# The attention stage of a decoder step: the order in which SyncE begins page loads, where the last eight value pages lie, and the place of the last gate half on TensorE

## The chip, the cores and the metric

The kernel runs as one program on one core of a Trainium2 chip. The metric is the device time of one execution in microseconds (us). The engines are named PE (TensorE), DVE (VectorE), ACT (ScalarE), POOL (GpSimd) and SP (SyncE, which here only begins transfers). PEld is the weight load of TensorE.

## The reference, cut to what matters

One step of a two-layer decoder trunk for a prompt of 512 tokens and 8 sample sequences of 4 tokens. In layer 0 a projection makes q, k, v, forget values and the inputs of a gated convolution. The prompt attends to itself; each sample sequence attends to its 16 cached pages (128 tokens each) and its own 4 tokens:

```
k_all = concat([k_pool[page_table].reshape(bsz, p_len, h, d), k_new], axis=1)
v_all = concat([v_pool[page_table].reshape(bsz, p_len, h, d), v_new], axis=1)
...
s = einsum('bqhd,bkhd->bhqk', q, k) * (HEAD_DIM ** -0.5) + (cq - ck)
p = softmax(s, axis=-1)
return einsum('bhqk,bkhd->bqhd', p, v)
```

An output projection, a ConvFFN, a Conformer convolution module and a second ConvFFN follow; the change does not touch them. Everything is float32; a product with a weight is made as three passes over high and low parts.

## The kernel before, in words

After the q, k, v projection comes a stage of NROUND = 20 rounds, written out in full for each engine. 8 sequences x 16 pages are 128 key pages and 128 value pages of 256 KB. Keys come in groups of GRP = 8 pages, in two buffers (k_grp, slots 0 and 1). Values come page by page, in eight buffers (v_pg). In round n the engines do this:

- PE scores key group n (score_group, L1898, for n < 16), counts it in s_sp, multiplies four value pages (value_page, L1952; the eight pages of a round are 8(n-4) to 8(n-4)+7) right behind it, turns the scores back (keys_back, L1906), scores the prompt's block 2n (block_score, L1969, counted in s_s), computes one or two gate halves (gate_half, L2019, 24 products each: half the columns of one slab of the convolution's projection), multiplies the other four value pages, and sums exponentials (exp_sums, L1937) and picks heads (own_heads, L1959). Each value page used is counted in s_pvp. Before a sequence's first value page PE waits until DVE has read the result of the sequence before (s_oev, counted by values, L1395), and multiplies its new values (L1948).
- DVE transposes key group n+1 in two halves (key_turned, L1262), reads scores and gate halves (L1414), makes sums.
- SP begins the transfers, in program order, each behind its own wait. In round n these are: the row cb of sums for a prompt head (L518, even rounds; it waits for DVE's L1324), the eight pages of key group n+2 (L457, waits s_sp >= n+1), in rounds 0 and 1 the outputs of turned rows, four value pages for PE's round n+1 (L467, each waits until its buffer's last page is counted in s_pvp), a gate weight in some rounds (L473), and the other four value pages.

Page ids are read from a table in SBUF into registers of SP, eight at a time, by page_id (L444), ahead of a group's first key page:

```
if n // GRP not in ids:
    ...
    ids[n // GRP] = nc.values_load_multi_w_load_instructions(
        page_row[0:1, at:at + GRP], engines=(mybir.EngineType.SP,), min_val=0, max_val=NPOOL - 1)[1]
```

Rounds 16 to 19 have no key groups. Round 17 computes the gate halves q = 21 and 22, round 18 the last one, 23. In round 18 PE uses value pages 112 to 119 and in round 19 pages 120 to 127; SP begins the latter behind s_pvp >= 113 to 120. Then the output projection starts (L1768 in `gemm(ph["out"], ...)`, behind L2091, which turns a small tail that DVE copies at L1508). POOL subtracts for the low part of its weights (L664), one slab after gate half 22, one after 23, one after s_pvp reaches 128.

Of the kernel before, what the change touches and what calls it, by code (L numbers as in the profile page):

```python
# [11 lines left out]
ds = bass.ds  # L12

P = 128
# [8 lines left out]
PG = 16  # L23
NPOOL = 160
# [9 lines left out]
KS, VS = 2, 8  # L34
# [6 lines left out]
NPAGE = NB * PG  # L41
GRP = 8
NGRP = NPAGE // GRP
LAG = 4
# [110 lines left out]
def build(nc, a, o):  # L155
# [6 lines left out]
    with ExitStack() as ctx:  # L162
# [58 lines left out]
        w_top = lambda at: at + 2 * DC * P * 4  # L221
        k_grp = [place(f"k_grp{n}", [P, GRP, 4 * P], F32, at)[0] for n, at in enumerate((R0, w_top(raw_at)))]
        own, _ = place("own", [P, P], F32, R0 + 16384)
        v_at = [w_top(wl_at) + n * 2048 for n in range(4)] + [R1, R1 + 2048, qkv_at + 11 * CH, ss_at + 6144]
# [98 lines left out]
        s_k = [[sem(f"k{n}_{half}") for half in range(2)] for n in range(KS)]  # L323
        s_v = [sem(f"v{n}") for n in range(VS)]
        s_ow, s_owr = sem("picked"), sem("picked_read")
        s_stc, s_clr, s_sel = sem("four_copied"), sem("banks_cleared"), sem("selectors")
# [79 lines left out]
        def _(sp):  # L406
# [31 lines left out]
            def page_id(n):  # L438

                if n // GRP not in ids:  # L440
                    if not ids:
                        sp.wait_ge(s_pg, 16)
                    at = n - n % GRP
                    ids[n // GRP] = nc.values_load_multi_w_load_instructions(  # L444
                        page_row[0:1, at:at + GRP], engines=(mybir.EngineType.SP,), min_val=0, max_val=NPOOL - 1)[1]
                return ids[n // GRP][n % GRP]
# [13 lines left out]
            def value_page(n):  # L460

                at = page_id(n)
                if n >= VS:
                    sp.wait_ge(s_pvp, n - VS + 1)
                elif n in (4, 5, 6, 7):
                    sp.wait_ge(s_kd[n - 4], 16)
# [57 lines left out]
            for n in range(NROUND):  # L524
                if n % 2 == 0 and n // 2 < NH:
                    head_cum(n // 2)
                if n + 2 < NGRP:
                    for j in range(GRP):
                        key_page(GRP * (n + 2) + j)
                for r in sum(ROWS_IN.get(n, ()), ()):  # L530
                    rows_written(r)
                values_at = GRP * (n - LAG + 1)
                if 0 <= values_at < NPAGE:
                    for j in range(4):
                        value_page(values_at + j)
                for q in halves_in(n):
                    if q % 2 == 0 and q // 2 + 2 < 12:
                        gate_load(q // 2 + 2)
                if 0 <= values_at < NPAGE:
                    for j in range(4, GRP):  # L540
                        value_page(values_at + j)
                if n == 15:
                    out_load(0)
# [1203 lines left out]
        def _(pe):  # L1747
# [192 lines left out]
            def value_page(n):  # L1940

                b, p = n // PG, n % PG
                if p == 0:
# [3 lines left out]
                    for c in range(4):  # L1947
                        mm(bank[0][32 * c:32 * c + 8, 0:P], pr[0:TS, b % 2, PG, c * 8:c * 8 + 8],  # L1948
                           s_row[:, 1, c * P:(c + 1) * P], start=True, stop=False)
                pe.wait_ge(s_v[n % VS], 16 * (n // VS + 1))  # L1950
                for c in range(4):
                    ins = mm(bank[0][32 * c:32 * c + 8, 0:P], pr[:, b % 2, p, c * 8:c * 8 + 8],  # L1952
                             v_pg[n % VS][:, c * P:(c + 1) * P], start=False, stop=p == PG - 1)
                ins.then_inc(s_pvp, 1)
# [74 lines left out]
            for n in range(NROUND):  # L2029
# [15 lines left out]
                for r in early:  # L2045
                    rows_turned(r)
                if values_at >= 0:
                    for j in range(4):
                        value_page(values_at + j)
# [13 lines left out]
                for r in late:  # L2063
                    rows_turned(r)
                for q in first:
                    gate_half(q, n)
# [185 lines left out]
```

## Time and profile before

| what | value |
| --- | --- |
| median of 3 runs | 1518.27 us (1516.08 to 1519.36) |
| profiled execution | 1527.78 us, its span 1525.9 us |
| PE busy | 1440.1 us (94%) |
| DVE, ACT, POOL busy | 744.6, 473.0, 587.1 us |
| mean granted clock of TensorE | 0.971 of full speed |
| DMA | 192.56 MB, mean 126 GB/s |

The profiled execution is 9.51 us above the median of the three runs. All positions in time below are microseconds from the start of its span. Busy time is the time in which an engine executes something; "idle before" is the gap ahead of an instruction, with what released it, and "issue" there means that the profile shows nothing the engine waited for.

### The profile page before, as it was taken

To read this page: it belongs to the slowest core of one execution; us is meant where nothing else is said; L and a number is where in the kernel's file an instruction comes from. 1 tells how busy PE (TensorE), PEld (TensorE's weight loads), DVE (VectorE), ACT (ScalarE), POOL (GpSimd) and SP (SyncE) were. 2 spreads that over 40 slices of the span, in tenths; PEclk is the share of its full clock that TensorE was granted. 3 is DMA by queue.
4 is the path that set the end of the run, shared out by engine and by line. 5 is a ranking of instruction groups with operands and counts; after the bars stand their busy time and mean duration, and the time that the engine had idled before them with its cause. 6 is when DMAs were issued, how large, how long until landed. Compare 5 with 4: busy or idle time off the path is not lost. (4 is left out here: it accounts for less than half of the span.)

```text
span 1525.9 us, 34946 instructions
## 1 busy us (share of the span) xinstructions
PE 1440.1 (94%) x13997; PEld 1326.6 (87%) x13997; DVE 744.6 (49%) x1258; ACT 473.0 (31%) x678; POOL 587.1 (38%) x321
## 2 busy tenths in 40 slices
PE   6998898899799999999999999986999999999998
PEld 5896666666689999999999987864999999999998
DVE  5654766677443544203443369988345441044411
ACT  5374222222134222312223331116443322222221
POOL 3312222222232645445444344430435444445441
PEclk9999988999989999999999999997999999999999
DMA  5416777987732332233322446560313323323222
GB/s 177 125 52 217 244 250 256 316 281 232 237 100 69 100 93 69 84 97 96 89 70 61 131 124 158 145 159 15 109 56 92 93 70 94 107 79 91 62 78 73
DMA packets 246375, 192.56 MB, mean 126 GB/s; under 512 B 12129, under 2 KB 205106, under 8 KB 246186
## 3 DMA queue, kind: packets, MB, share of 16 engines
q1 hardware_dynamic: 244753, 188.71, 40.6%
q10 hardware_dynamic: 1373, 1.84, 0.5%
q8 instruction: 77, 1.26, 0.3%
q0 software_dynamic: 144, 0.52, 0.1%
q14 instruction: 28, 0.23, 0.0%
HBM read 173.03 MB, written 6.04 MB: 117 GB/s over the span
## 5 line engine op out<-in xcount | busy, mean ns | idle before, releaser
L664 POOL TENSOR_TENSOR w_l<-w_raw,w_h 128x1024 fp32r<-128x1024 f32 (+2 forms) x195 | 432.9, 2222 | 447.6 <-ACT w_h L791 418.8
L1768 PE MATMUL banks<-xa_h,w_h 128*128 128x272 f32 x1856 | 388.2, 290 | 4.5 <-DVE tmp L1590 3.3
L1768 PE MATMUL banks<-xa_h,w_l 128*128 128x272 f32 x1856 | 384.9, 289 | 0.0
L1768 PE MATMUL banks<-xa_l,w_h 128*128 128x272 f32 x1856 | 383.6, 288 | 0.0
L1768 PEld LDWEIGHTS banks<-xa_h,w_h 128*128 128x128 f32 x1856 | 293.3, 189 | 6.8 <-issue 5.5
L1768 PEld LDWEIGHTS banks<-xa_l,w_h 128*128 128x128 f32 x1856 | 292.6, 189 | 0.0
L1768 PEld LDWEIGHTS banks<-xa_h,w_l 128*128 128x128 f32 x1856 | 290.5, 189 | 0.0
L791 ACT ACTIVATE w_h<-w_raw 128x1024 fp32r<-128x1024 f32 (+2 forms) x193 | 185.1, 961 | 182.5 <-PE banks L1768 182.2
L1768 PE MATMUL banks<-h_h,w_h 128*128 128x272 f32 x960 | 202.4, 292 | 8.1 <-DVE h_l L1737 8.0
L1768 PE MATMUL banks<-h_h,w_l 128*128 128x272 f32 x960 | 200.7, 291 | 0.0
L1768 PE MATMUL banks<-h_l,w_h 128*128 128x272 f32 x960 | 200.2, 290 | 0.0
L1529 DVE TENSOR_TENSOR x<-banks,x 128x544 f32 (+1 forms) x48 | 34.8, 725 | 271.5 <-PE banks L1768 271.5
L1768 PEld LDWEIGHTS banks<-h_h,w_h 128*128 128x128 f32 x960 | 153.2, 191 | 10.0 <-issue 7.5
L1768 PEld LDWEIGHTS banks<-h_l,w_h 128*128 128x128 f32 x960 | 153.2, 191 | 0.0
L1768 PEld LDWEIGHTS banks<-h_h,w_l 128*128 128x128 f32 x960 | 152.0, 191 | 0.0
L738 POOL TENSOR_TENSOR sr<-sl,r_all 128x544 f32<-128x544 f32 x44 | 59.8, 1360 | 232.8 <-ACT sl L1022 232.8
L1022 ACT ACTIVATE sl<-cv 128x544 f32<-128x544 f32 x44 | 29.0, 659 | 276.8 <-DVE cv L1585 276.7
L685 POOL TENSOR_SCALAR sb<-sb,small 128x128 f32<-128x128 f32 (+3 forms) x32 | 34.7, 1083 | 180.0 <-DVE small L1336 180.0
L1152 DVE TENSOR_TENSOR gate<-banks,r_all 128x544 f32<-128x544 f32 x44 | 31.8, 724 | 110.5 <-PE banks L1768 104.7
L1590 DVE TENSOR_TENSOR tmp<-banks,sr 128x544 f32<-128x544 f32 x44 | 31.9, 725 | 107.5 <-POOL sr L738 107.5
L1262 DVE STREAM_TRANSPOSE k_grp<-k_grp 128x2048 f32<-128x2048 f32 x32 | 73.5, 2298 | 0.4 <-DMA k_grp<-in_cache_k 0.4
L1576 DVE SCALAR_TENSOR_TENSOR cv<-gate,params,cv 128x511 f32<-128x511 f32 x88 | 66.1, 751 | 12.7
(286 smaller groups left out, 1698.4 us busy)
## 6 DMA issues: line engine op xcount, KB each, us to landing
w_raw<-in_w_up SPq DMA_DIRECT2D x88, 512.0 KB, 3.6
k_grp<-in_cache_k SPq DMA_DIRECT2D x128, 256.0 KB, 4.1
v_pg<-in_cache_v SPq DMA_DIRECT2D x128, 256.0 KB, 5.2
w_raw<-in_w_in SPq DMA_DIRECT2D x24, 512.0 KB, 6.5
w_raw<-in_w_down SPq DMA_DIRECT2D x32, 384.0 KB, 3.1
w_raw<-in_w_pw SPq DMA_DIRECT2D x24, 512.0 KB, 4.1
w_raw<-in_w_down SPq DMA_DIRECT2D x32, 320.0 KB, 3.1
w_raw<-in_w_out SPq DMA_DIRECT2D x8, 512.0 KB, 6.3
```

What stands on the lines that cost most here:

```text
L664: g.tensor_tensor(w_l[:, slot, 0:n], w_raw[:, slot, 0:n], w_h[:, slot, 0:n].bitcast(F32), ALU.subtract).then_inc(s_lo, 1)
L685: g.tensor_scalar(sb[:, k % 2, 0:n], sb[:, k % 2, 0:n], rinv[:, w:w + 1], None, ALU.mult).then_inc(s_pn, 1)
L738: g.tensor_tensor(sr[:, j // 2, :], sl[:, j // 2, :], r_all[:, :], ALU.mult)\
L791: A(w_h[:, slot, 0:n], w_raw[:, slot, 0:n], ACT.Copy).then_inc(s_hi, 1)
L1022: A(sl[:, b, :], cv[:, b, :], ACT.Silu).then_inc(s_sl, 1)
L1152: V.tensor_tensor(halves(dst), gview(b), halves(r_all[:, :]), ALU.mult).then_inc(s_free, 1)
L1262: V.transpose(k_grp[slot][:, at, :].rearrange("p g x -> p (g x)"), k_grp[slot][:, at, :].rearrange("p g x -> p (g x)")).then_inc(s_tk, 1)
L1529: V.tensor_tensor(halves(flat(x[:, ds(m, 1), :])), gview(q % 2), halves(flat(x[:, ds(m, 1), :])), ALU.add).then_inc(s_xnew, 1)
L1576: V.scalar_tensor_tensor(yp, gate[:, b, 0:TP - n], w, yp, ALU.mult, ALU.add)\
L1590: V.tensor_tensor(halves(tmp[:, b, :]), gview(1), halves(sr[:, b, :]), ALU.mult).then_inc(s_free, 1)
L1768: ins = mm(out[:, half, 0:HT], w, v[:, half * HT:(half + 1) * HT], start=first and t == 0 and n == 0, stop=last and t == phase.tiles - 1 a ...
```

## The change

It has four parts.

1. page_id reads the same ids, and leaves out the check of each against 0 and 159.
2. In each round SP's order becomes: four key pages, the turned rows (rounds 0 and 1), four value pages, then a wait for s_s >= 2n+1 (the prompt's block 2n is scored), the other four key pages, the gate weight, the other four value pages.
3. Value pages 120 to 127 go to v_last, which is key buffer 0, free once group 14 is scored (s_sp >= 15). SP begins them in round 15. PE waits for them in two lots of four.
4. Gate half 23 stands ahead of the first value page of round 18 on PE.

```diff
+        v_last = k_grp[(NGRP - 2) % KS]
...
+        s_vl = [sem(f"v_last{n}") for n in range(2)]
...
                     ids[n // GRP] = nc.values_load_multi_w_load_instructions(
-                        page_row[0:1, at:at + GRP], engines=(mybir.EngineType.SP,), min_val=0, max_val=NPOOL - 1)[1]
+                        page_row[0:1, at:at + GRP], engines=(mybir.EngineType.SP,), min_val=0, max_val=NPOOL - 1,
+                        skip_runtime_bounds_check_because=...)[1]
...
                 at = page_id(n)
+                if n >= NPAGE - GRP:
+                    sp.wait_ge(s_sp, NGRP - 1)
+                    sp.dma_start(v_last[:, n % GRP, :], a["cache_v"][0, ds(at, 1)].rearrange("a k h d -> (a k) (h d)"))\
+                      .then_inc(s_vl[n % GRP // 4], 16)
+                    return
...
-                if n + 2 < NGRP:
-                    for j in range(GRP):
-                        key_page(GRP * (n + 2) + j)
-                for r in sum(ROWS_IN.get(n, ()), ()):
-                    rows_written(r)
-                values_at = GRP * (n - LAG + 1)
-                if 0 <= values_at < NPAGE:
-                    for j in range(4):
-                        value_page(values_at + j)
-                for q in halves_in(n):
-                    if q % 2 == 0 and q // 2 + 2 < 12:
-                        gate_load(q // 2 + 2)
-                if 0 <= values_at < NPAGE:
-                    for j in range(4, GRP):
-                        value_page(values_at + j)
+                values_at = GRP * (n - LAG + 1)
+                for half in range(2):
+                    if half and n + 2 < NGRP:
+                        sp.wait_ge(s_s, 2 * n + 1)
+                    if n + 2 < NGRP:
+                        for j in range(4 * half, 4 * half + 4):
+                            key_page(GRP * (n + 2) + j)
+                    if not half:
+                        for r in sum(ROWS_IN.get(n, ()), ()):
+                            rows_written(r)
+                    else:
+                        for q in halves_in(n):
+                            if q % 2 == 0 and q // 2 + 2 < 12:
+                                gate_load(q // 2 + 2)
+                    if 0 <= values_at < NPAGE - GRP:
+                        for j in range(4 * half, 4 * half + 4):
+                            value_page(values_at + j)
                 if n == 15:
+                    for j in range(GRP):
+                        value_page(NPAGE - GRP + j)
                     out_load(0)
...
-                pe.wait_ge(s_v[n % VS], 16 * (n // VS + 1))
+                if n < NPAGE - GRP:
+                    pe.wait_ge(s_v[n % VS], 16 * (n // VS + 1))
+                else:
+                    pe.wait_ge(s_vl[n % GRP // 4], 64)
+                page = v_pg[n % VS] if n < NPAGE - GRP else v_last[:, n % GRP, :]
...
+                if n == NROUND - 2:
+                    half_read(last_half(n, 1))
+                    for q in first:
+                        gate_half(q, n)
                 if values_at >= 0:
                     for j in range(4):
                         value_page(values_at + j)
...
-                for q in first:
+                for q in first if n < NROUND - 2 else ():
                     gate_half(q, n)
```

The order of SP's instructions at the start of round 4 before the change; cb is the row of sums, k_grp a key page, "ISA x16" the sixteen instructions of the check, "ISA" ahead of a key page its address:

```order
L518 DMA cb<-cum_rows 128x512 [waits p_read]
L444 TENSOR_LOAD page_row
L444 ISA x16
L457 ISA [waits page_scored]
L457 DMA k_grp_86<-in_cache_k 128x512
```

The same engine from there on with the change, up to the fifth key page (the row with "p_scored" is the new wait):

```order
L527 DMA cb<-cum_rows 128x512 [waits p_read]
L446 TENSOR_LOAD page_row
L461 ISA [waits page_scored]
L461 DMA k_grp_86<-in_cache_k 128x512
...
L476 DMA v_pg_89<-in_cache_v 128x512 [waits page_valued]
L476 DMA v_pg_90<-in_cache_v 128x512 [waits page_valued]
L476 DMA v_pg_91<-in_cache_v 128x512 [waits page_valued]
L476 DMA v_pg_92<-in_cache_v 128x512 [waits page_valued]
L461 ISA [waits p_scored]
L461 DMA k_grp_86<-in_cache_k 128x512
```

The check's sixteen instructions are gone and the first four value pages stand between the two halves of the key group.

PE in rounds 18 and 19 before the change, with buffer names (v_pg0 to v_pg7 the value pages, s_row the new values; the rows of L2019 are products of gate half 23, of which 24 stand there):

```order
L1948 MATMUL banks<-s_row_84,pr_72 8x128 x4
L1952 MATMUL banks<-v_pg0_89,pr_72 8x128 x4
L1952 MATMUL banks<-v_pg1_90,pr_72 8x128 x4
L1952 MATMUL banks<-v_pg2_91,pr_72 8x128 x4
L1952 MATMUL banks<-v_pg3_92,pr_72 8x128 x4
L2019 MATMUL banks<-xa_h_50,w_h_55 128x288
...
L1952 MATMUL banks<-v_pg4_93,pr_72 8x128 x4
```

And with the change, from the same place to the end of the stage:

```order
L2036 MATMUL banks<-xa_h_50,w_l_56 128x288
L1961 MATMUL banks<-s_row_84,pr_72 8x128 x4
L1969 MATMUL banks<-v_pg0_89,pr_72 8x128 x4
...
L1969 MATMUL banks<-v_pg7_96,pr_72 8x128 x4
L1950 MATMUL banks<-ones_58,small_77 8x1 x4
L1976 MATMUL banks<-small_77,own_88 128x16
L1969 MATMUL banks<-k_grp0_86,pr_72 8x128 x32
```

The gate half stands ahead of the new values' products, and the last eight pages are read from the key buffer in one piece of 32 products.

## Rows read from the trace of the kernel before

**Rows 1.** The page: busy us by engine; one group: busy, mean ns | idle before.
```profile
PE 1440.1 (94%) x13997; PEld 1326.6 (87%) x13997; DVE 744.6 (49%) x1258; ACT 473.0 (31%) x678; POOL 587.1 (38%) x321
...
L664 POOL TENSOR_TENSOR w_l<-w_raw,w_h 128x1024 fp32r<-128x1024 f32 (+2 forms) x195 | 432.9, 2222 | 447.6 <-ACT w_h L791 418.8
```

**Rows 2.** Stretches: us, busy PE, PEld, DVE, ACT, POOL, PEclk, DMA share, GB/s.
```profile
203.90:223.60 19.70, 17.13 (x240) 11.79 (x239) 9.97 (x20) 3.43 (x8) 3.27 (x3) 0.74 0.84 291
223.60:238.50 14.90, 14.31 (x277) 10.91 (x276) 11.46 (x22) 4.25 (x8) 3.70 (x3) 1.00 0.73 239
238.50:258.40 19.90, 16.71 (x240) 11.42 (x239) 11.68 (x24) 3.54 (x8) 4.07 (x4) 0.74 0.85 287
...
287.10:306.70 19.60, 16.58 (x281) 12.70 (x283) 11.75 (x22) 4.31 (x8) 4.50 (x3) 0.83 0.87 300
306.70:319.90 13.20, 12.87 (x243) 8.68 (x244) 9.31 (x19) 3.32 (x8) 3.27 (x3) 1.00 0.68 222
319.90:337.30 17.40, 15.69 (x277) 12.30 (x276) 11.62 (x22) 4.85 (x9) 3.72 (x3) 0.90 1.03 352
...
350.20:368.20 18.00, 16.02 (x277) 12.28 (x276) 12.53 (x23) 4.25 (x8) 3.98 (x3) 0.91 0.63 217
424.90:430.00 5.10, 5.10 (x30) 5.10 (x29) 3.73 (x6) 2.67 (x5) 2.35 (x1) 0.66 0.35 106
```

**Rows 3.** PE's timeline, rounds 5 and 14: start, duration, row, [idle before].
```profile
210.17 0.61 PE L1952 MATMUL banks<-v_pg,pr 128*8 128x128 f32 x6 [2.57 <-issue]
...
350.17 2.62 PE L1898 MATMUL banks<-k_grp,q_blk 32*8 32x256 f32 x122
354.51 0.61 PE L1898 MATMUL banks<-k_grp,q_blk 32*8 32x256 f32 x6 [1.72 <-issue]
```

**Rows 4.** DMA queues between 350.0 and 352.5: packets, MB, share of 16 engines.
```profile
q1 hardware_dynamic: 1068, 0.92, 107.2%
q8 instruction: 1, 0.02, 2.2%
```

**Rows 5.** SP's timeline in round 4, then the instructions of L444.
```profile
191.12 0.33 SPq L518 DMA_DIRECT2D cb<-cum_rows  x1
194.27 5.24 SPq L457 DMA_DIRECT2D k_grp<-in_cache_k  x8
199.61 4.26 SPq L467 DMA_DIRECT2D v_pg<-in_cache_v  x8
...
L444 SPq FUSED_REGOPS  x128: 147/147/188, 43.0 to 338.7; - x128
```

**Rows 6.** PE's timeline, rounds 17 to 19 and the first product of the output projection.
```profile
396.29 0.37 PE L2019 MATMUL banks<-xa_h,w_h 128*128 128x288 f32 x1 [0.91 <-DVE sc_b L1372]
...
399.55 0.28 PE L2019 MATMUL banks<-xa_h,w_h 128*128 128x256 f32 x1
...
407.36 0.40 PE L1948 MATMUL banks<-s_row,pr 32*8 32x128 f32 x8 [3.83 <-DVE own L1395]
...
414.50 0.21 PE L1937 MATMUL banks<-ones,small 128*8 128x1 f32 x8
...
414.97 1.06 PE L1952 MATMUL banks<-v_pg,pr 128*8 128x128 f32 x32
417.51 0.41 PE L1952 MATMUL banks<-v_pg,pr 128*8 128x128 f32 x8 [1.49 <-DMA v_pg<-in_cache_v]
...
421.05 0.61 PE L1952 MATMUL banks<-v_pg,pr 128*8 128x128 f32 x8 [1.60 <-DMA v_pg<-in_cache_v]
...
424.89 0.80 PE L1768 MATMUL banks<-h_h,w_h 128*128 128x272 f32 x2
```

**Rows 7.** DVE's timeline in round 17.
```profile
406.75 0.47 DVE L1395 TENSOR_SCALAR own<-banks,small 128x64 f32<-128x64 f32 x2
```

**Rows 8.** Value pages begun by SP between 403.4 and 404.7.
```profile
L467 SPq DMA_DIRECT2D v_pg<-in_cache_v x3: 379/379/380, 403.4 to 404.3; - x3
...
DMA to landing us min/median/max: 4.3/4.5/4.7
```

More of the change, by code:

```diff
@@ L444, in page_id @@
                     ids[n // GRP] = nc.values_load_multi_w_load_instructions(
-                        page_row[0:1, at:at + GRP], engines=(mybir.EngineType.SP,), min_val=0, max_val=NPOOL - 1)[1]
+                        page_row[0:1, at:at + GRP], engines=(mybir.EngineType.SP,), min_val=0, max_val=NPOOL - 1,
+                        skip_runtime_bounds_check_because="a page table holds ids of the pool's pages, and each page's "
+                                                          "DMA checks its address by itself")[1]
                 return ids[n // GRP][n % GRP]
@@ L526, in _ @@
                     head_cum(n // 2)
-                if n + 2 < NGRP:
-                    for j in range(GRP):
-                        key_page(GRP * (n + 2) + j)
-                for r in sum(ROWS_IN.get(n, ()), ()):
-                    rows_written(r)
-                values_at = GRP * (n - LAG + 1)
-                if 0 <= values_at < NPAGE:
-                    for j in range(4):
-                        value_page(values_at + j)
-                for q in halves_in(n):
-                    if q % 2 == 0 and q // 2 + 2 < 12:
-                        gate_load(q // 2 + 2)
-                if 0 <= values_at < NPAGE:
-                    for j in range(4, GRP):
-                        value_page(values_at + j)
-                if n == 15:
+                values_at = GRP * (n - LAG + 1)
[15 more added lines that the diff above has]
+                            value_page(values_at + j)
+                if n == 15:
+                    for j in range(GRP):
+                        value_page(NPAGE - GRP + j)
                     out_load(0)
@@ L1949, in value_page @@
                            s_row[:, 1, c * P:(c + 1) * P], start=True, stop=False)
-                pe.wait_ge(s_v[n % VS], 16 * (n // VS + 1))
+                if n < NPAGE - GRP:
[3 more added lines that the diff above has]
+                page = v_pg[n % VS] if n < NPAGE - GRP else v_last[:, n % GRP, :]
                 for c in range(4):
                     ins = mm(bank[0][32 * c:32 * c + 8, 0:P], pr[:, b % 2, p, c * 8:c * 8 + 8],
-                             v_pg[n % VS][:, c * P:(c + 1) * P], start=False, stop=p == PG - 1)
+                             page[:, c * P:(c + 1) * P], start=False, stop=p == PG - 1)
                 ins.then_inc(s_pvp, 1)
```

## The prediction

> **What bounds the kernel now.** First the page: PE is busy 94% of the span, so it is the bound nearly everywhere [rows 1]. What a change to SP's queue can bring are PE's remaining gaps and what they cost behind them. Next the stretches by round: PE's work repeats every two rounds, and rounds of one kind should last alike. They don't. Odd round 11 takes 13.20 us, odd rounds 5 and 7 take 19.70 and 19.90; even round 6 takes 14.90, rounds 10, 12 and 14 take 19.60, 17.40 and 18.00 [rows 2]. Over the undisturbed round of their kind that is 6.5, 6.7, 4.7, 2.5 and 3.1, together 23.5 us. In the long rounds the granted clock averages 0.74 to 0.91, in rounds 6 and 11 it is 1.00: a gap is followed by a stretch at the lower of the two levels.
>
> Then PE's timeline at such a gap: in round 5 it stands 2.57 us before the last products of a value quartet, "issue"; in round 14 it stands 1.72 us after 122 of the 128 equal products of one score group, where no semaphore is waited for at all [rows 3]. So something other than data is late. The DMA queues just before show the ordinary queue at 107% of 16 engines, and beside it one packet of the instruction queue; its 2.2% of 16 engines over 2.5 us are 0.9 us [rows 4]. I read it as PE's instructions arriving late through engines that are full of pages. The score group, with a weight load for each of its 128 products in 2.6 us, is where PE uses up instructions fastest, and the gap falls in or just behind it.
>
> Last the end of the stage: PE stands 3.83 us for DVE's `own` before round 18, 1.49 and 1.60 us for the last value pages, and starts the output projection at 424.89 [rows 6].
>
> **The end of the stage (parts 3 and 4).** Before, PE is through with round 17 at 407.36 - 3.83 = 403.53 and starts the projection at 424.89, 21.36 us later [rows 6]. After, step by step: at 403.53 gate half 23 follows; its twin, half 21, took 399.55 - 396.29 = 3.26 [rows 6], so 406.79. Its bank was freed in round 17 before `own`, in DVE's order. `own` is written at 406.75 to 407.22 [rows 7] and PE went on at 407.36 then, and will again: 0.57 of the 3.83 us stay. New values 0.40 and two quartets of 1.06 (the row at 414.97) give 409.88 at full clock; the small products 414.97 - 414.50 = 0.47 give 410.35 [rows 6]; eight pages in one piece, 2 x 1.06, give 412.47. From there to the projection, own_heads, DVE's tail and L2091 stay as they were: before, 424.89 - (421.05 + 0.61) = 3.23. Sum 415.70, against 424.89: **9.2 us** gained.
>
> What hides what: pages 120 to 127 are begun in round 15, some 20 us ahead of use, so their landing is covered. Pages 116 to 119 are not moved, and are now wanted at 408.8: they were begun by 404.3 and landed in 4.3 to 4.7, so at 409.0 for the last [rows 8]; PE uses it as the fourth, at 409.6, with 0.6 to spare. POOL's subtraction behind half 23 starts beside DVE's `own` now. Should they hinder each other, the loss is one POOL operation, 2.2 us on the mean [rows 1]. Eight more page loads stand ahead of SP's first output weight and of pages 104 to 107: 8 x 0.38 = 3.0 us by the issue time of a page [rows 8]. Those four pages were begun about a round ahead of use (13.2 us or more [rows 2]), and the output weights are split only in rounds 17 and 18, so I price both at nothing. Bounds of the end: 9.2 - 2.2 - 0.6 = 6.4 below; above, the projection's first 5.10 us ran at 0.66 [rows 2], and would at full clock be 1.7 shorter: 10.9.
>
> **The ids (part 1).** The check goes: 16 of the instructions of each group, 8 of which take 0.147 us, so at least 1.2 us a group [rows 5]. The gap between cb's end at 191.45 and the first key page at 194.27 is 2.8 us, and holds the load of ids too [rows 5]; I take 2.0 off it. SP is on no path by itself. What moves is when the DMA engines get their work: in even rounds 2 us sooner. In odd rounds the ids are read ahead of the wait for the scores, and little moves.
>
> **The bursts (part 2).** Before, the value pages of round 4 were begun in one run from 199.61 to 203.87 [rows 5], 2 MB in front of round 5's score group and its gap at 207.6 (210.17 - 2.57). With the change four of them are begun in front of the second half of the keys, at about 194.27 - 2.0 + 5.24/2 = 194.9, and only the four that wait for PE's second quartet remain. So about 1 MB less, and everything 2 us sooner, is in the engines when PE's instructions run short. The bytes are the same, and the rate stays near what the engines give: 287 to 352 GB/s in long rounds [rows 2]. That is why I don't expect every gap to go; in rounds as close as 10 and 12 the pages of one round meet those of the next however they are ordered. The new wait, s_s >= 2n+1, holds up behind it four key pages, the gate weight and the last value quartet. The quartet waits for PE anyway, and later; the keys' second half is turned by DVE in the middle of the next round; half a round (6.6 us or more) stands between, and 4 pages need 2.6 of it on SP (half of 5.24 [rows 5]) and 4.7 to land [rows 8], begun in the first third of the round before. Nobody waits.
>
> Its worth outside the profile: the three runs have a median 9.51 below the profiled one, so of the 23.5 us perhaps 14.0 are there at all. Rounds 5 and 7, where the runs of pages shrink, hold 13.2/23.5 = 56%, 7.9 us. Between nothing and 7.9 I take half, **4.0 us**.
>
> The Trainium skill speaks against this term: Runtime: NRT & Kernel Launch, section Instruction fetch mechanics, says that the sequencer streams 16 KiB blocks by its own DMA queue and that this is mostly hidden. The size agrees with the 0.02 MB packet [rows 4]; by its rule the gaps of rows 3 are no fetches, and SP's order would bring nothing.
>
> Sum: 1518.27 - 9.2 - 4.0 = 1505.1 us. In the profiled execution it would be 1527.78 - 13.2 = 1514.6, or less if rounds 5 and 7 lose all 13.2.
>
> **Rivals.**
> - *All gaps of the rounds go.* 14.0 instead of 4.0: 1495.1; from 7.9, 1501.2. For it: the gaps are tied to a full queue. Against: rounds 10, 12, 14 keep as many bytes per us.
> - *Only the end gains.* PE's gaps have another cause, or shift with the pages: 1509.1. For it: no row shows the packet's own wait, and whether a round is hit looks like chance (11 is not). The rule above gives this case.
> - *The end gains little.* Another wait takes the place of the 3.83 us, such as pages 116 to 119 or `own` behind POOL; only the 3.1 us for the last pages are won, and nothing in the rounds: 1515.2. For it: the margin of 0.6 us. Against: it would have to eat the whole gate half.
> - *Slower: the spread pages meet PE's instructions in every round.* Now pages are begun in four places, and one lot follows PE's first quartet directly. A hit costs 6.5 us (round 5). The end's 9.2 are used up from the second additional hit on; four more would be 26 - 9 = 17 slower, 1535; two more, 1522. For it: rounds 6 and 11 run at full clock now and have something to lose. Against: fewer pages in a lot, and those begun earlier.
>
> **How the numbers follow.** Likeliest, 0.44: end and half of the two rounds, 1505.1, its own range 1501.2 to 1509. All or most gaps go: 0.22 (1495 to 1501). Only the end: 0.22 (1509 to 1512 with its lower bound, 1518.3 - 6.4 = 1511.9). End gains little: 0.07 (1512 to 1517). Slower: 0.05. The range 1496 to 1512 leaves out a small part of the second case and the last two, under 0.2. Within 0.2% (about 3 us, what a measurement of this kernel can tell) means 1515.2 to 1521.3: 0.04, from the fourth case and the mildest hits. Faster: 0.92. Slower: 0.04.
>
> **What the profile after would show.** PE goes from half 23's last product to the new values with under 1 us idle; pages 120 to 127 as one run of about 2.1 us with no idle for DMA; the projection starts some 9 us nearer to the end of round 17. In the rounds, the first key page of even rounds is begun within 1 us of cb's end, and rounds 5 and 7 last nearer to 13.2 than to 19.7 with the clock at 1.00. I am wrong if PE shows new idle before the quartets of rounds 16 to 18, if DVE's transpositions wait for keys, or if the "issue" gaps keep their number and only stand elsewhere.

## The result, and the profile after

| | before | with the change |
| --- | --- | --- |
| median, timed side by side (6 runs each) | 1517.17 us | 1502.2 us |
| profiled execution, its span | 1527.78, 1525.9 us | 1501.65, 1499.7 us |
| mean granted clock | 0.971 | 0.982 |
| start of round 4's score group | 189.51 | 188.16 |
| PE through with round 17 | 403.53 | 393.99 |
| start of the output projection | 424.89 | 405.36 |
| from there to the end of the span | 1101.0 | 1094.3 |

The ratio of the two kernels' times is 0.9913, its 95% interval [0.9885, 0.9941]: faster by 13.2 us (9.0 to 17.4). The medians in the table lie 15.0 apart; gains below are by the ratio unless medians are named. The two profiled executions lie 26.2 us apart in their spans. The table splits this: 1.35 ahead of round 4, 8.2 in rounds 4 to 17 (214.0 to 205.8), 10.0 from there to the projection (21.36 to 11.37), 6.7 behind it. The last is in code that the change doesn't touch. In the profiled executions of the experiments below it is 1092 to 1095, and 1100.9 in one: I count it as scatter between executions and no part of the gain.

First the page, against [rows 1]. PE does the same 13997 products in 12.8 us less, at a mean clock that is a little higher:

```profile
PE 1427.3 (95%) x13997; PEld 1317.4 (88%) x13997; DVE 712.8 (48%) x1258; ACT 473.0 (32%) x678; POOL 590.7 (39%) x321
```

PE's timeline from round 17 to the projection, against [rows 6] (start, duration, row, idle before). The first row is the last value quartet of round 17; 24 products of the gate half follow it, of which the first and the last stand here.

```profile
392.93 1.06 PE L1969 MATMUL banks<-v_pg,pr 128*8 128x128 f32 x32
393.92 0.40 PE L2036 MATMUL banks<-xa_h,w_h 128*128 128x288 f32 x1
...
397.09 0.29 PE L2036 MATMUL banks<-xa_h,w_l 128*128 128x288 f32 x1
397.88 0.40 PE L1961 MATMUL banks<-s_row,pr 32*8 32x128 f32 x8 [0.50 <-DVE own L1408]
398.21 2.01 PE L1969 MATMUL banks<-v_pg,pr 128*8 128x128 f32 x64
400.04 0.21 PE L1950 MATMUL banks<-ones,small 128*8 128x1 f32 x8
...
400.50 1.93 PE L1969 MATMUL banks<-k_grp,pr 128*8 128x128 f32 x64
403.04 0.40 PE L1976 MATMUL banks<-small,own 128*128 128x16 f32 x2 [0.60 <-DVE own L1408]
404.99 0.61 PE L2112 MATMUL banks<-ident,tail_a 128*18 128x128 f32 x4 [1.56 <-DVE tail_a L1521]
405.36 0.50 PE L1781 MATMUL banks<-h_h,w_h 128*128 128x272 f32 x2
```

The gate half stands where PE stood 3.83 us; 0.50 us of that wait is left. The four pages 116 to 119 follow without a gap, and so do pages 120 to 127: the three waits for DMA of [rows 6], 1.49 and 1.60 among them, are gone.

SP's timeline in round 4, against [rows 5]: a burst of eight key pages and one of eight value pages have become four of four, and the first key page is begun 0.90 us behind cb's end (191.00 - 190.10), where it was 2.82. It can't be begun sooner now, because it waits for round 4's scores, which end at 188.16 + 2.67 = 190.83.

```profile
189.77 0.33 SPq L527 DMA_DIRECT2D cb<-cum_rows  x1
191.00 1.88 SPq L461 DMA_DIRECT2D k_grp<-in_cache_k  x4
192.98 1.80 SPq L476 DMA_DIRECT2D v_pg<-in_cache_v  x4
195.59 2.12 SPq L461 DMA_DIRECT2D k_grp<-in_cache_k  x4
199.65 1.76 SPq L476 DMA_DIRECT2D v_pg<-in_cache_v  x4
```

Rounds 5, 6, 7, 10, 12 and 14, against [rows 2] (us, busy PE, PEld, DVE, ACT, POOL, granted clock, DMA share, GB/s), and behind them the first 5.1 us of the projection:

```profile
202.50:215.80 13.30, 12.71 (x241) 8.71 (x240) 10.01 (x20) 3.43 (x8) 3.27 (x3) 1.00 0.83 291
215.80:233.90 18.10, 15.71 (x284) 11.98 (x290) 11.67 (x22) 4.25 (x8) 3.78 (x3) 0.91 0.93 310
233.90:247.40 13.50, 12.53 (x240) 8.58 (x239) 11.45 (x24) 3.54 (x8) 3.95 (x4) 1.00 0.82 283
277.90:297.50 19.60, 16.77 (x282) 12.73 (x285) 11.74 (x22) 4.31 (x8) 4.50 (x3) 0.83 0.83 277
310.70:326.50 15.80, 14.09 (x277) 10.93 (x276) 11.67 (x22) 4.85 (x9) 3.70 (x3) 1.00 1.06 394
339.40:357.20 17.80, 16.08 (x283) 11.73 (x287) 12.61 (x23) 4.25 (x8) 4.04 (x3) 0.90 0.63 216
405.40:410.50 5.10, 5.10 (x31) 5.10 (x30) 3.73 (x6) 2.95 (x5) 2.08 (x1) 0.67 0.36 106
```

Rounds 5 and 7 are down from 19.70 and 19.90 to 13.30 and 13.50. But round 6 is up from 14.90 to 18.10 and round 8 from 15.1 to 16.7. Of the 12.8 us that two rounds gave, 4.8 went back in the rounds behind them. Whether the change did this is asked below, under "The same code, other rounds".

PE's gaps in rounds 5, 6 and 14, against [rows 3]. Each gap stands before the last products of a group of equal ones, and waits for no semaphore:

```profile
205.12 1.04 PE L1969 MATMUL banks<-v_pg,pr 128*8 128x128 f32 x26
206.75 0.40 PE L1969 MATMUL banks<-v_pg,pr 128*8 128x128 f32 x6 [0.59 <-issue]
...
219.08 0.84 PE L1969 MATMUL banks<-v_pg,pr 128*8 128x128 f32 x22
222.04 1.01 PE L1969 MATMUL banks<-v_pg,pr 128*8 128x128 f32 x10 [2.13 <-issue]
...
339.63 2.37 PE L1911 MATMUL banks<-k_grp,q_blk 32*8 32x256 f32 x102
343.47 0.61 PE L1911 MATMUL banks<-k_grp,q_blk 32*8 32x256 f32 x6 [1.46 <-issue]
```

An fp32 product leaves two such rows of products, so a quartet of pages has 32 and a score group 128. Count rows from the start of a round's score group (even rounds have 16 more rows between scores and pages, odd rounds none). In rounds 6, 8, 10, 12 and 14 the gap stands after 166, 155, 144, 133 and 122 rows; in rounds 5, 7 and 9 after 154, 143 and 132. Every two rounds it comes 11 rows earlier, in the kernel before too, and no data is due at such places. Rounds 4 and 11 have small ones of the same kind (0.3 to 0.4 us after 176 and 120 rows). Only the lengths differ: 0.59, 2.13, 0.97, 2.08, 1.07, 2.57, 1.44 and 1.46 us for rounds 5 to 10, 12 and 14, where before it was 2.57, 0.33, 3.19, 0.48, 0.74, 2.75, 1.44 and 1.72.

What PE waits for can be read from the DMA view. In rounds 5 to 14 of the kernel before (203.88 to 368.23) the instruction queue moved 21 packets of 16 KB, while PE left 2576 records of products and as many of weight loads (first the queue's line, then that of the window):

```profile
q8 instruction: 21, 0.34, 0.8%
203.88:368.23 164.35, 148.98 (x2576) 108.32 (x2576) 112.35 (x208) 40.19 (x83) 38.32 (x30) 0.90 0.81 276
```

That is one packet for 5152 / 21 = 245 PE instructions, two packets a round. Narrow windows of the same view give the moment at which a packet begins. The last one ahead of each gap's end:

| round | before: packet begins, PE goes on | with the change |
| --- | --- | --- |
| 5 | 207.75, 210.17 | 204.26, 206.75 |
| 6 | 225.64, 228.05 | 219.58, 222.04 |
| 7 | 242.57, 244.94 | 235.80, 238.03 |
| 14 | 352.06, 354.51 | 341.21, 343.47 |

Every time PE goes on 2.2 to 2.5 us after the packet began. The same holds for 85 of the 87 gaps of this kind of 0.2 us and more between 200 and 360 us in the traces of all kernels of this document (the other two: 2.85 and 3.11, behind packets that took 1.4 and 1.6 us; the median packet of the kernel before takes 0.95). So the gaps are PE waiting for its own instructions, and a gap is longer the later its packet begins.

### The profile page after: what moved, and what is told of

The parts are those of the page before. It is cut to its first block, busy times and chain, and to the rows that moved or that the text cites. A ratio compares the mean times of both kernels' runs of the same rounds, so it can differ in the third digit from the quotient of the medians.

```text
span 1499.7 us, 34690 instructions
## 1 busy us (share of the span) xinstructions
PE 1427.3 (95%) x13997; PEld 1317.4 (88%) x13997; DVE 712.8 (48%) x1258; ACT 473.0 (32%) x678; POOL 590.7 (39%) x321
## 4 chain that ended last, share of the span: by engine, by line
PE 84%; DVE 7%; issue 3%; ACT 3%; DMA 1%; POOL 1%; SPq 0%; ACTq 0%; DVEq 0%; POOLq 0%
PE banks L1781 65%; PE banks L2036 5%; PE banks L2203 2%; PE banks L1911 2%; PE banks L1969 2%; PE banks L2009 1%; PE banks L1986 1%; PE banks L1919 1%; DVE k_grp L1275 1%; DVE suf L1217 1%; PE banks L1813 1%; DVE ssum L1183 1%; PE banks L1996 1%; PE banks L2155 0%; DMA x_rows<-in_x_sample 0%
## 5 line engine op out<-in xcount | busy, mean ns | idle before, releaser
L677 POOL TENSOR_TENSOR w_l<-w_raw,w_h 128x1024 fp32r<-128x1024 f32 (+2 forms) x195 | 439.1, 2253 | 429.5 <-ACT w_h L804 408.8
L1589 DVE SCALAR_TENSOR_TENSOR cv<-gate,params,cv 128x511 f32<-128x511 f32 x88 | 66.1, 751 | 12.8
```

What stands on the lines that cost most here:

```text
L677: g.tensor_tensor(w_l[:, slot, 0:n], w_raw[:, slot, 0:n], w_h[:, slot, 0:n].bitcast(F32), ALU.subtract).then_inc(s_lo, 1)
L1589: V.scalar_tensor_tensor(yp, gate[:, b, 0:TP - n], w, yp, ALU.mult, ALU.add)\
```

## The experiments

Each kernel was timed against the kernel before on the same chip, and the ratios have 95% intervals. Three groups were each timed together: end_only, rounds_only, after_shift128 and before_shift128 (before: 1515.14 us); ids_only, bursts_only, after_light_pages and after_shift64 (1515.96); the last four (1515.33). Parts are numbered as in the section on the change.

**The end alone and the rounds alone.** end_only has parts 3 and 4 (pages 120 to 127 into v_last, gate half 23 first), rounds_only has parts 1 and 2.

```diff
 end_only: before, with
+                    sp.dma_start(v_last[:, n % GRP, :], ...).then_inc(s_vl[n % GRP // 4], 16)
+                if n == NROUND - 2:
+                    half_read(last_half(n, 1))
+                    for q in first:
+                        gate_half(q, n)
 rounds_only: before, with
+                        skip_runtime_bounds_check_because=...
+                    if half and n + 2 < NGRP:
+                        sp.wait_ge(s_s, 2 * n + 1)
```

> Parts 3 and 4 alone: pages 120 to 127 in the key buffer, gate half 23 ahead of round 18's values; the ids are checked and SP keeps the order of before. My theory (the end is worth about 9.2 us by itself, measured 10.0 between the two profiled executions, the rest of the gain comes from the rounds): 8 to 11 us faster than before, and in the profile the same 11.4 us from the end of round 17 to the first product of the output projection as in the changed kernel; rounds 5 and 7 as long as before (19 to 20 us) if the profile catches them so. Rival (the whole gain is the end, the rounds only scatter): 12 to 14 us faster.

> Parts 1 and 2 alone: unchecked ids and four bursts a round; the last pages and the last gate half stay as before. My theory: 2 to 6 us faster than before, with the end's 21.4 us unchanged. Rival (the end alone gains): within 1.5 us of before. Rival (spreading the pages meets more instruction fetches): slower by 2 us or more.

end_only: 1506.23 us, 0.9933 [0.9908, 0.9958], 10.1 us faster. rounds_only: 1510.78 us, 0.9968 [0.9947, 0.999], 4.8 us faster. Together 14.9, where the whole change gave 13.2 (9.0 to 17.4): within the intervals the two halves add up, and each has about the size that the forecast gave it. In end_only's trace the stretch from the end of round 17 to the projection is 11.32 us, as expected. Its rounds 5 and 7 last 20.15 and 15.25 us, the second far from the 19.90 of before, though nothing in them differs from the kernel before. In rounds_only PE still stands 3.83 us for `own` ahead of round 18:

```profile
394.71 0.52 PE L1954 MATMUL banks<-s_row,pr 32*8 32x128 f32 x8 [3.83 <-DVE own L1401]
```

**PE's instructions moved against the rest.** If blocks of instructions arrive late, the gaps belong to places in PE's instruction stream, and padding ahead of them must move them. after_shift128 puts 32 products of one column ahead of PE's wait for the input, where PE stands idle anyway; each fp32 product is four PE instructions (two weight loads, two products), so 128. before_shift128 does the same to the kernel before.

```diff
             pe.wait_ge(s_cst, 15)
+            for _ in range(32):
+                mm(bank[1][0:8, 0:1], ones[:, 0:8], ones[:, 0:1], start=True, stop=True)
             pe.wait_ge(s_gin, 16)
```

> The changed kernel with 32 one-column products ahead of everything else on PE, while it waits for its first data: 128 instructions more, half a block of 16 KB, and nothing else moves. Theory that the issue gaps are late instruction blocks: every gap stands 64 product records earlier in the program (in round 14 after about 58 of the 128 score products instead of 122; in round 10, where it stood ahead of all 32 value products, after about 64 of the score group or just before), and since a block's fetch then has slower instructions in front of it than the score group alone, the gaps get shorter: together under 6 us instead of 12.3, and 4 to 12 us faster than the changed kernel, 17 to 25 faster than before. Rival (the gaps are waits for pages or semaphores that the profile doesn't name): gaps at the same products as before, and the time of the changed kernel, about 13 us under before.

> The kernel before with the same 32 one-column products at PE's start, 128 instructions, nothing else. Theory of late instruction blocks: gaps 64 product records earlier and shorter, 5 to 13 us faster than before, without any part of the change. Rival (waits for data): same gaps at the same products, within 1.5 us of before.

after_shift128: 1483.13 us, 0.9767 [0.9736, 0.9797], 35 us faster than before (32 by the medians) and about 19 faster than the change (by the medians, 1502.2 - 1483.1). before_shift128: 1494.12 us, 0.9847 [0.9818, 0.9876], 23 us (21 by the medians) with no part of the change in it. Both gains lie well above what was expected, 17 to 25 and 5 to 13. The windows of before_shift128's rounds 5, 6, 7 and 10:

```profile
202.70:215.50 12.80, 12.74 (x247) 8.63 (x252) 10.04 (x20) 3.42 (x8) 3.27 (x3) 1.00 0.98 345
215.50:229.70 14.20, 13.93 (x280) 10.81 (x283) 11.42 (x22) 4.25 (x8) 3.76 (x3) 1.00 1.00 340
229.70:242.50 12.80, 12.43 (x240) 8.50 (x239) 11.77 (x24) 3.31 (x8) 3.99 (x4) 1.00 0.95 327
270.10:284.40 14.30, 14.03 (x286) 10.91 (x293) 11.62 (x23) 4.31 (x8) 4.50 (x3) 1.00 0.96 331
```

These are the strongest rows of the study. The DMA engines are as full as ever (0.95 to 1.00, 327 to 345 GB/s), PE does the same work, and rounds 5, 6, 7 and 10 last 12.8, 14.2, 12.8 and 14.3 us instead of 19.7, 14.9, 19.9 and 19.6, all at full clock. The full queue alone takes next to nothing from PE in these rounds; what costs is where a block of instructions ends. Not every gap is gone: in before_shift128 one of 1.45 us is left in round 14, and one of 0.24 in round 13. In after_shift128 one gap of 1.07 us is left in round 14, in the products that turn the scores back:

```profile
329.49 0.82 PE L1921 MATMUL banks<-ident,s_t 128*128 128x128 f32 x6
331.38 0.38 PE L1921 MATMUL banks<-ident,s_t 128*128 128x128 f32 x2 [1.07 <-issue]
```

The expectation said that the gaps stand 64 rows earlier. Here they can't be found, since they are gone, but the last kernel with this padding (without_bursts_shift128, below) still has three: in round 5 after 91 rows (154 - 64 = 90), and in round 14 after 59 (122 - 64 = 58) and after 185. The last two:

```profile
326.71 1.66 PE L1911 MATMUL banks<-k_grp,q_blk 32*8 32x256 f32 x69 [0.92 <-issue]
...
332.24 0.38 PE L1919 MATMUL banks<-ident,s_t 128*128 128x128 f32 x2 [1.07 <-issue]
```

Why does the place matter? The gaps of rounds 5 and 6 stand 241 - 154 + 166 = 253 rows apart, those two in round 14 only 185 - 59 = 126. With one packet for about 245 instructions this fits boundaries 128 rows (256 instructions with the weight loads) apart, of which mostly every second one shows. Then one fell shortly after round 5's score group had started (154 - 128 = 26) and the next shortly after its end. So 102 of a block's 128 rows were scores, of which 128 take 2.67 us: it was used up fast. With padding that moves it by 64 rows the boundary falls into the middle of the scores (90), and the blocks on both sides hold slower work. In before_shift128 the packet ahead of that place began at 201.94, before the score group of round 5 did (202.70). That the time in which a block is used up decides is my reading of these positions. Against its simplest form stands the next kernel, whose boundaries at 123 and 125 rows make blocks of almost nothing but scores, and which is still faster than the change. No record shows when a block's transfer is asked for.

after_shift64 has half of the padding:

```diff
+            for _ in range(16):
+                mm(bank[1][0:8, 0:1], ones[:, 0:8], ones[:, 0:1], start=True, stop=True)
```

> The changed kernel with 16 one-column products at PE's start, 64 instructions. Late-block theory: boundaries stand 32 product records earlier than in the changed kernel, in round 14 after 90 of the 128 score products; the block that is used up while the next one is fetched holds 96 of the score group's products and 32 slower ones, so the gaps are shorter than in the changed kernel and not gone: 1484 to 1498. Rival (only whether there is a shift matters, or chance): the time of the changed kernel, or of the one shifted by 128.

1491.91 us, 0.9846 [0.9817, 0.9875], between the two, as expected. The gaps came 31 rows earlier (32 expected, and a count of rows may be off by one): round 5 from 154 to 123, round 6 from 166 to 135, round 10 from 144 to 113. Four are left (round 8 has the fourth, 1.35 us), and from round 11 on there is none. The rows of PE's timeline in rounds 5 and 6:

```profile
200.88 2.62 PE L1913 MATMUL banks<-k_grp,q_blk 32*8 32x256 f32 x123
205.04 0.60 PE L1913 MATMUL banks<-k_grp,q_blk 32*8 32x256 f32 x5 [1.53 <-issue]
...
222.46 0.39 PE L1932 MATMUL banks<-q_diag,qkv 128*32 128x8 f32 x7
224.82 0.17 PE L1932 MATMUL banks<-q_diag,qkv 128*32 128x8 f32 x1 [1.97 <-issue]
```

**The engines emptied.** after_light_pages keeps every transfer and wait, but from a buffer's second use on a page brings 16 rows of 128 columns instead of 128 of 512, so the attention over pages computes from other values.

```diff
-                sp.dma_start(k_grp[slot][:, i, :], ...)
+                k, w = (P, 4 * P) if grp < KS else (16, P)
+                sp.dma_start(k_grp[slot][0:k, i, 0:w], ...[0:k, 0:w])
```

> The changed kernel, but from the second use of each buffer on a key or value page brings only its first 16 rows of 128 columns (8 KB of 256 KB); the rest of the buffer keeps what lay there, so the attention over cached pages is computed from wrong pages. Same instructions, same waits, same number of transfers. Theory (instruction blocks arrive late because the DMA engines are full of pages): all issue gaps of rounds 5 to 14 go (under 0.5 us in sum, 12.3 in the changed kernel), rounds last 12.3 to 14.3 us, the time is that of the shifted kernel or a little under, 1478 to 1486. Rival (a block's fetch is slow whatever else is moved): gaps stay, time within 4 us of the changed kernel, about 1502.

1476.8 us, 0.974 [0.9709, 0.9771], a little under what was expected. Rounds 5, 6, 7 and 10:

```profile
202.70:215.30 12.60, 12.60 (x244) 8.73 (x246) 10.05 (x20) 3.39 (x8) 3.27 (x3) 1.00 0.18 45
215.30:229.80 14.50, 14.23 (x280) 10.90 (x282) 11.47 (x22) 4.25 (x8) 3.75 (x3) 1.00 0.15 39
229.80:242.70 12.90, 12.59 (x241) 8.62 (x240) 11.77 (x24) 3.31 (x8) 3.98 (x4) 1.00 0.18 42
269.20:283.70 14.50, 14.03 (x277) 10.85 (x276) 11.45 (x22) 4.31 (x8) 4.50 (x3) 1.00 0.16 46
```

With the DMA engines at 0.15 to 0.18 these rounds last 12.6 to 14.5 us at full clock, and of the gaps 0.32 (round 7) and 0.20 (round 10) are left. So a long gap needed both, a boundary in the wrong place and full engines. Round 5 shows how. Its packet begins 3.9 us behind the start of the score group before the change (207.75 - 203.88), 1.8 with it (204.26 - 202.51), and 1.2 with light pages (203.92 - 202.73). PE comes to the 154th row 3.7 us behind that start (207.60 - 203.88), and a packet serves it 2.2 to 2.5 us after its beginning: with light pages that is just in time. From round 4's scores to the projection this kernel takes 195.3 us, after_shift128 197.5, before_shift128 208.9, the change 217.2 and the kernel before 235.4. By these traces padding leaves 2.2 us of what empty engines could give, by the ratios about 4 (0.9767 against 0.974).

**Parts 1 and 2 apart.** ids_only is the kernel before without the check of ids, bursts_only the kernel before with SP's new order and the wait for s_s.

```diff
 ids_only: before, with
+                        skip_runtime_bounds_check_because=...
 bursts_only: before, with
+                for half in range(2):
+                    if half and n + 2 < NGRP:
+                        sp.wait_ge(s_s, 2 * n + 1)
+                    ... (four key pages, ..., four value pages)
```

> Part 1 alone: ids read unchecked, SP's order of before. My step: the key pages of even rounds begin about 2 us sooner, nothing else. Alone it should bring 0 to 2.5 us. Rival (the spread of the pages does all the work, the check was hidden behind waits): within 1 us of before. Rival (the check is the whole of the rounds' gain): 3 to 6 us faster.

> Part 2 alone: four bursts a round, ids checked. My step: it carries most of the 4.8 us that both parts brought in the rounds: 2 to 5 us faster than before, rounds 5 and 7 near 13 to 16 us. Rival (the check's removal is what counts): within 1 us of before.

ids_only: 1509.69 us, 0.996 [0.994, 0.998], 6.1 us faster (3.0 to 9.1). That is more than the 0 to 2.5 expected, and nearer to the rival that the check is the whole of the rounds' gain. bursts_only: 1517.95 us, 1.0017 [0.9995, 1.0038]: 2.6 us slower by the ratio, not told from no change, and a gain above 0.8 us is outside the interval. It was expected 2 to 5 us faster; that was a miss. A caution on profiles stands here too: bursts_only's profiled execution is the fastest of its 12 (1508.51; the others 1514.56 to 1525.19), ids_only's the slowest of its 11 (1518.26; the others 1506.02 to 1513.09). One trace of each would have ranked them the wrong way round, so a term of a few us in the gaps can't be read from one execution.

**The same code, other rounds.** In the result rounds 5 and 7 were 6.4 us shorter and 6 and 8 longer. Did the bursts do it? ids_only has SP's order of before, and its rounds 5 to 8 last 13.54, 21.03, 13.10 and 19.98 us. last_pages_only (below) differs from the kernel before only from round 15 on, and its trace has for rounds 5 to 8:

```profile
201.34:215.41 14.07, 12.71 (x241) 8.71 (x240) 10.01 (x20) 3.43 (x8) 3.27 (x3) 1.00 0.89 311
215.41:231.86 16.45, 14.33 (x277) 10.92 (x276) 11.62 (x22) 4.26 (x8) 3.73 (x3) 1.00 0.93 319
231.86:245.45 13.59, 12.59 (x241) 8.62 (x240) 11.55 (x24) 3.54 (x8) 4.03 (x4) 1.00 0.87 297
245.45:265.20 19.75, 17.12 (x277) 12.86 (x276) 12.46 (x23) 4.97 (x9) 4.00 (x3) 0.83 0.80 278
```

So SP's program of before gives short rounds 5 and 7 and a long 8 in this execution, and 19.70, 19.90 and 15.1 in the other. With one trace of each kernel, neither the shorter rounds 5 and 7 of the changed kernel nor its longer 6 and 8 can be put down to the change.

**The change without its bursts.**

```diff
-                for half in range(2):
-                    ...
+                if n + 2 < NGRP:
+                    for j in range(GRP):
+                        key_page(GRP * (n + 2) + j)
+                ... (SP's order of before, last eight value pages still in v_last)
```

> The changed kernel without part 2: ids unchecked, last pages in the key buffer, gate half 23 moved, SP in the order of before (eight key pages, four values, gate weight, four values). Theory after the first runs (part 1 brings about 6 us, the end 10, part 2 nothing): 14 to 18 us faster than before, no slower than the changed kernel (13.2). Rival (parts 1 and 2 need each other in the full change): 9 to 12 us faster, some 2 to 4 slower than the changed kernel.

> The same with the 32 one-column products at PE's start. Theory: with the block boundaries out of the score groups the order of SP's bursts is worth nothing either way: 1480 to 1486, within 3 us of the changed kernel so shifted (1483.1). Rival (bursts matter once the fetches are out of the way, through pages that land late): more than 3 us apart, with idle ahead of value products put down to DMA v_pg.

without_bursts: 1497.93 us, 0.9877 [0.9844, 0.991], 18.6 us faster than before, where the full change has 13.2. The intervals overlap (0.9885 to 0.9941 for the full change, timed apart), so it isn't settled whether the bursts do harm; it is the third comparison that shows them no help (bursts_only against before +2.6 us; rounds_only against ids_only +1.2 us and the full change against this one +5.5 us, both from kernels timed apart). without_bursts_shift128, the same with 32 padding products: 1480.77 us, 0.9769 [0.9741, 0.9796], equal to after_shift128 (0.9767). Once the blocks end elsewhere, SP's order makes no difference that can be measured here (each interval reaches about 4 us either way). These two are the best versions with the reference's work, 35 us faster than before and about 20 faster than the change.

**Parts 3 and 4 apart.** gate_only moves gate half 23 alone, last_pages_only has the eight pages in v_last alone; their diffs are the two halves of end_only's.

> Part 4 alone: gate half 23 ahead of round 18's values. By my steps it fills 3.26 of the 3.83 us idle and spares the slow clock behind it (about 1.5 us of products at the lower level), while the last pages still wait for PE: 3 to 6 us faster than before; the waits for the last pages stay, 3 to 4 us of idle put down to DMA v_pg, or grow, since less work stands between the pages' release and their use: 4 page pairs now follow round 18 at once. Rival (the two parts only work together, the pages' wait takes back what the gate gives): within 2 us of before.

> Part 3 alone: pages 120 to 127 in the key buffer, gate half 23 where it was. By my steps the DMA waits of the last pages go (1.49, 0.23, 1.60 us) and some products run at the higher clock: 3 to 6 us faster than before, the 3.83 us for own stay. Rival: the eight pages begun in round 15 delay pages 104 to 107 or the output weights, and the gain is under 2 us.

gate_only: 1512.53 us, 0.998 [0.9961, 1.0], 3.0 us faster. PE's timeline from the new values on:

```profile
414.62 0.40 PE L1950 MATMUL banks<-s_row,pr 32*8 32x128 f32 x8 [0.45 <-DVE own L1397]
...
418.21 0.41 PE L1955 MATMUL banks<-v_pg,pr 128*8 128x128 f32 x8 [0.97 <-DMA v_pg<-in_cache_v]
420.10 3.23 PE L1955 MATMUL banks<-v_pg,pr 128*8 128x128 f32 x40 [1.49 <-DMA v_pg<-in_cache_v]
423.87 1.25 PE L1955 MATMUL banks<-v_pg,pr 128*8 128x128 f32 x16 [0.54 <-DMA v_pg<-in_cache_v]
```

The wait for `own` is 0.45, and PE is sooner at pages that aren't sooner there: it waits 0.97, 1.49 and 0.54 for them, and has their products at the lower clock.

last_pages_only: 1511.99 us, 0.9977 [0.9956, 0.9998], 3.5 us faster. The same stretch:

```profile
396.36 0.40 PE L1957 MATMUL banks<-s_row,pr 32*8 32x128 f32 x8 [3.77 <-DVE own L1404]
...
403.93 1.93 PE L1965 MATMUL banks<-k_grp,pr 128*8 128x128 f32 x64
409.34 0.61 PE L1972 MATMUL banks<-small,own 128*128 128x16 f32 x2 [3.47 <-DVE own L1404]
```

The 3.77 us ahead of the row at 396.36 stay, the pages are there in one piece, and then PE waits 3.47 us for DVE's last `own`, where it was 0.60. Alone the parts are worth 3.0 + 3.5 = 6.5 us, together 10.1; the intervals (0 to 5.9, 0.3 to 6.7, 6.4 to 13.9) can't tell this from a plain sum. The traces speak against one. From the end of round 17 to the projection it is 21.36 us before (20.3 to 21.6 in the other kernels without these two parts), 17.57 in gate_only (428.36 - 410.79), 17.87 in last_pages_only (410.46 - 392.59) and 11.32 in end_only: 3.8 and 3.5 us alone, 10.0 together. Some of the gap that each removes is taken back by the other's wait.

## Why the prediction was right, and where it wasn't

The time was forecast at 1505.1 us, 13.2 below the median; measured were 13.2 (9.0 to 17.4) by the ratio and 1502.2 us by the median. The likeliest case gave the right time. Its term for the end was right for its reasons; its term for the rounds was right in size by luck.

**The end of the stage: right.** Forecast 21.36 to 12.17 us (415.70 - 403.53), measured 11.37, and 10.1 us (6.4 to 13.9 by the interval) in end_only. The steps held: the wait for `own` shrank to 0.50 (0.57), DMA waits vanished, pages 116 to 119 came in time, the projection started right behind. POOL's 2.2 us for a hindered `own` were not paid. PE was 0.8 us quicker than summed: about 0.5 because rows that I added end to end overlap (the new values and two quartets took 2.16 and not 2.52, the last pages 1.93 and not 2.12), and 0.3 between the last product and the projection (2.93 against 3.23). The upper bound by a faster projection wasn't had: its first 5.1 us still ran at 0.67. That part 3 and part 4 need each other was in the sum only silently, since it was worked out for both at once.

**The ids: right in place, too small in worth.** 1.9 us came off the gap behind cb (2.0 forecast). But the forecast gave this part no price of its own; alone it is worth 6.1 us (3.0 to 9.1), more than the whole term of the rounds. By which path it gains them no trace shows: ids_only's gaps stand at the same rows as before.

**The bursts: wrong, and this is the step that failed.** "About 1 MB less ... is in the engines when PE's instructions run short" was to shorten rounds 5 and 7. They were shorter, by 6.4 each in the profile, and I had named that as a sign of being right. It is none: last_pages_only has rounds 5 and 7 at 14.07 and 13.59 with SP's order of before. The gaps kept their number and their products to the row, and alone the part gave nothing (1.0017 [0.9995, 1.0038]). The sign that I named as a refutation, gaps that keep their number, was met in its first half. The term of the rounds, 4.0, agreed with the measured 4.8 (1.5 to 8.0) by luck: the ids gave what the bursts didn't.

**The cause of the gaps: right, its size too small.** That PE's instructions arrive late through full DMA engines is what three things show: the gaps moved by 31 rows with 64 instructions of padding, they are nearly gone with light pages, and each ends 2.2 to 2.5 us after a packet of the instruction queue begins. The packet of [rows 4] is one of these: it begins at 352.06, and PE goes on at 354.51. The Trainium skill, Runtime: NRT & Kernel Launch, section Instruction fetch mechanics, holds the fetch to be mostly hidden; for 9 of the 21 blocks in rounds 5 to 14 of the kernel before it wasn't, at 0.3 to 3.2 us each with full engines. I priced all gaps at 14.0 us outside the profile, and padding alone took 21 to 23 us from the kernel before. The mis-sized step is the 9.51 us by which the profiled execution was longer, which I took wholly off the gaps. Some 7 us of them lie behind the projection's start, where that execution took 1101.0 us and all others but one 1092 to 1095. The rounds themselves were priced nearly right: 23.5 us, and rounds 5 to 14 went from 164.4 us to 137.8 with padding.

**The rivals.** All gaps go: no, they kept number and place. Only the end gains: no, rounds_only has 1.5 to 8.0 us without the end, though its verdict on SP's order, that it brings nothing, is what bursts_only shows. The end gains little: no, it gained 10.1. Slower: no; rounds 6 and 8 were longer in this profile, but that comes with SP's order of before too.

**The profiled execution** was forecast at 1514.6 and came at 1501.65. The 13 us between: 4.2 more in the rounds, 0.8 at the end, 1.4 ahead of round 4, 6.7 behind the projection's start. That one execution of before was long there says how little a single profile is worth as a base.

What stays open: whether the bursts cost some us or nothing, how the ids gain their 6.1 us, and when the transfer of a block is asked for.

## What to carry to other kernels

An idle engine with no semaphore behind it, in the midst of equal instructions, at a place that moves by the same number of rows from round to round, was here a block of instructions arriving late, and such gaps are worth looking for where the DMA queues are full; the instruction queue's packets in the DMA view settle it. Then padding of a few dozen tiny products in a stretch where the engine waits anyway can move the boundaries off the densest stretch: 21 to 23 us here for nothing, more than a reordering of the transfers. How much padding is right has to be tried: 64 instructions gave half of what 128 gave. A round that is shorter in one trace proves nothing until the same code has been seen to keep its rounds. Edits that take two waits from one short stretch are to be priced and made together: alone these two took 7.3 us off it, together 10.0.

## What the runs showed of the hardware

- PE's instructions come in 16 KB packets on a queue of their own (21 in a stretch with 5152 PE instructions). In 85 of 87 gaps PE went on 2.2 to 2.5 us after a packet had begun. The packet itself took no longer with full engines (median 0.95 us between 200 and 360 in the kernel before) than with light pages (1.08); with full ones it began later.
- The places where PE runs dry have a fixed spacing in its instruction stream. Two rounds hold 517 to 525 rows of products in the windows, and the gap comes 11 rows earlier every two rounds, as it would if it came every 512; 64 instructions ahead of it moved it by 31 rows.
- Full DMA engines alone hardly slow PE: 327 to 345 GB/s beside rounds of 12.8 to 14.3 us at full clock, where empty engines have 12.6 to 14.5.
- A gap of 2 to 3 us costs more than itself. Round 7 of before had one of 3.19 and was 6.4 us longer than the same round with 0.97; its clock averaged 0.74 against 1.00. A gap of 1.44 in round 12 came with a round of 17.4 us at 0.90 before and 15.8 at 1.00 after, so the same gap need not cost the same.
- The check of a group of eight ids costs at least 1.9 us on SP's queue (2.82 against 0.90 behind cb); the kernel without it was 6.1 us faster (3.0 to 9.1), by a path that no trace here shows.
